# Two column blocks of the modulation matrix read in two-row pieces and multiplied on four column strips, in a one-core kernel of two transformer blocks

## What is computed

```python
# first block: a vector c modulates the block, nine vectors of 1024
mod = silu(c) @ w_ada + b_ada            # w_ada is 1024 x 9216
sh1, sc1, gt1, sh2, sc2, gt2, sh3, sc3, gt3 = split(mod, 9)
u = rmsnorm(h, g_norm_ffn1) * (1 + sc1) + sh1
h = h + 0.5 * gt1 * swiglu(u, w_ffn1_in, w_ffn1_out)
...                                       # mixing, second FFN, final norm
# second block, two layers: mixer, layer norm, routed experts, layer norm
x = layer_norm(ALPHA * x + mixer(x), ln1_g, ln1_b)
f = hier_moe(x)      # 1 of 8 groups, then 2 of its 8 experts for each token
x = layer_norm(ALPHA * x + f, ln2_g, ln2_b)
```

## Time and profile before

| | us |
|---|---|
| median of three runs | 2788.43 (2787.32 to 2788.45) |
| the profiled execution | 2787.28 |
| its span | 2785.5 |
| PE busy | 2512.2 (90%) |
| PE weight loads busy | 1814.7 (65%) |
| DVE busy | 1378.5 (49%) |
| ACT busy | 822.7 (30%) |
| POOL busy | 97.8 (4%) |

### The profile page before, as it was taken

How to read it: one execution, slowest core, us unless ns; L and a number is a source line. 1 busy time by engine, 2 the same in 40 slices (tenths; PEclk the granted TensorE clock), 3 DMA queues, 4 the chain that set the end, 5 groups by cost and what they waited for, 6 DMA issues and landing times.

```text
span 2785.5 us, 37631 instructions
## 1 busy us (share of the span) xinstructions
PE 2512.2 (90%) x14755; PEld 1814.7 (65%) x14756; DVE 1378.5 (49%) x2444; ACT 822.7 (30%) x1400; POOL 97.8 (4%) x80
## 2 busy tenths in 40 slices
PE   6999999999999999999788888888999968888886
PEld 5888888777678888787645444445765854444443
DVE  4655744634452225544664443434966475444444
ACT  3222334256232224322222112122367332121121
POOL 0100002000000000000020000003000020000000
PEclk8999999999999999999899999999999989999999
DMA  7655432401232332223389999984230449999976
GB/s 251 191 188 190 160 98 84 139 31 61 106 106 91 105 98 83 91 91 121 136 328 422 422 422 422 422 347 153 76 107 1 151 152 408 421 421 422 422 302 283
DMA packets 206763, 593.78 MB, mean 213 GB/s; under 512 B 9472, under 2 KB 133584, under 8 KB 157264
## 3 DMA queue, kind: packets, MB, share of 16 engines
q1 hardware_dynamic: 202880, 575.47, 53.9%
q0 software_dynamic: 3504, 16.63, 1.9%
q10 hardware_dynamic: 288, 0.42, 0.1%
HBM read 590.32 MB, written 7.41 MB: 215 GB/s over the span
## 4 chain that ended last, share of the span: by engine, by line
PE 65%; DMA 22%; DVE 7%; ACT 3%; issue 2%; SPq 1%; DVEq 0%; ACTq 0%
PE bank L1950 39%; DMA arena<-in_exp_w 19%; PE bank L2306 6%; PE bank L2040 4%; DMA ring<-in_exp_w 2%; PE bank L2326 1%; PE bank L2533 1%; SPq L580 1%; PE bank L2211 1%; PE bank L2430 1%; PE bank L2500 1%; DMA ring<-in_w_ada 1%; PE bank L2130 1%; DVE ring_low L1207 1%; PE bank L2275 1%
## 5 line engine op out<-in xcount | busy, mean ns | idle before, releaser
L1950 PE MATMUL bank<-parts 128*128 128x512 f32 x2624 | 816.9, 393 | 15.2 <-DVE parts L1256 9.7
L1950 PEld LDWEIGHTS bank<-parts 128*128 128x128 f32 x2624 | 492.8, 189 | 117.2 <-issue 14.8
L1950 PE MATMUL bank<-parts,ring_low 128*128 128x512 f32 x1312 | 513.4, 391 | 0.0
L1207 DVE TENSOR_TENSOR ring_low<-ring,parts 128x2048 fp32r<-128x2048 f32 x106 | 238.1, 2250 | 215.2 <-ACT parts L770 214.9
L2306 PE MATMUL bank<-ring,arena 128*32 128x256 f32 x2112 | 290.5, 433 | 57.8 <-DMA arena<-in_exp_w 57.8
L2306 PE MATMUL bank<-arena 128*32 128x256 f32 x2112 | 290.7, 433 | 30.8 <-issue 30.8
L1950 PEld LDWEIGHTS bank<-parts,ring_low 128*128 128x128 f32 x1312 | 247.7, 189 | 52.2
L770 ACT ACTIVATE parts<-ring 128x2048 fp32r<-128x2048 f32 x106 | 198.9, 1877 | 263.5 <-DMA ring<-in_w_ffn_in 108.6
L2306 PEld LDWEIGHTS bank<-ring,arena 128*32 128x32 f32 x2112 | 139.3, 120 | 122.7 <-issue 94.7
L2333 PE MATMUL bank<-parts 128*128 128x512 f32 x496 | 169.3, 447 | 43.8 <-DVE parts L1699 22.9
L1950 PE MATMUL bank<-ring_low 128*128 128x512 f32 x576 | 194.4, 396 | 1.7 <-ACT arena L1008 1.7
(11 more groups left out here) (349 smaller groups left out, 3548.4 us busy)
## 6 DMA issues: line engine op xcount, KB each, us to landing
arena<-in_exp_w SPq DMA_DIRECT2D x192, 1024.0 KB, 18.1
ring<-in_exp_w SPq DMA_DIRECT2D x192, 1024.0 KB, 18.9
ring<-in_w_ffn_in SPq DMA_DIRECT2D x44, 1024.0 KB, 6.8
ring<-in_w_ada SPq DMA_DIRECT2D x36, 1024.0 KB, 5.2
ring<-in_w_ffn_out SPq DMA_DIRECT2D x20, 1024.0 KB, 5.1
ring<-in_w_in SPq DMA_DIRECT2D x18, 1024.0 KB, 5.0
ring<-in_conv_w_in SPq DMA_DIRECT2D x12, 1024.0 KB, 5.1
ring<-in_attn_w_in SPq DMA_DIRECT2D x10, 1024.0 KB, 5.3
```

The costliest lines, as they stand in the source:

```text
L1207: TTn(ring_low[:, n, 0:nk * cols], ring[:, n, 0:nk * cols], buf.bitcast(F32), ALU.subtract)\
L1950: i = mm(o, a[:, cols[0], cols[1]], b, start=first_ and n == 0, stop=last_ and n == 2)
```

## The change

Four things are edited together.

1. *Prologue.* The eight first chunks of `w_ada` become two row tiles by 1024 columns (rows of 4 KB), four for `sc1` and then four for `sh1`. PE takes all of them: the stationary operand is a 32-column tile `CZ` whose first column is the silu vector and the rest zero, the chunk is the moving operand in halves of 512 columns, and the four products of a chunk fall on four different column strips. Of two banks, DVE copies the sums to `AROW`, and PE adds over partitions with a column of ones, eight products for a vector. PE's order becomes: chunks 0 and 1, transposes of `x`, chunks 2 and 3, the norm's spread, the sums of `sc1`, chunks 4 to 7, the sums of `sh1`. DVE writes all eight `U` tiles between the two vectors, then the low weights, then the low tiles. The stream's order of chunks stays as it was; the chunks are freed by PE's semaphore `ada_mm`.
2. *Token layout.* `XTH` and `XTL` keep the tokens' own column order, so that ACT and DVE read and write runs; the regrouping moves to `rows`, where PE's transposes read every eighth float of `XG`, and so wait for both halves of it.
3. *Layer norm.* For the last token tile DVE scales before it writes the former tile's half, and PE transposes the last tile before it takes the former tile's logits.
4. *Plan.* DVE's `rows_high` of the first turn is placed within the plan, and the last copy of the plan goes.

```diff
+        AROW = area(11264, 2, 512)
+        CZ = area(8192, KT, 32)
...
-                used = ("ada_mm", a + 1) if a < ADA_FIRST and a % 2 else ("ada_step", steps_before(a) + 8)
-                stream_a.append((tall(A["w_ada"], 256 * a, 256), KT, 256, *used))
+                if a < ADA_FIRST:
+                    stream_a.append((flat(A["w_ada"], 2 * (a % 4), 2, D * (1 - a // 4), D), 2, D, "ada_mm", a + 1))
+                else:
+                    stream_a.append((tall(A["w_ada"], 256 * a, 256), KT, 256, "ada_step", steps_before(a) + 8))
...
@@ ACT, norm @@
                     weights_high(0)
                     weights_high(1)
+                    act.wait_ge(sem("ada_mod"), ADA_FIRST)
...
             def rounded_tokens(j, t):
                 act.wait_ge(sem("xn"), 4 * j + t + 1)
-                evac(grouped(XTH, t), byrow(t), "xt")
+                evac(XTH[:, t], HT[:, t], "xt")
...
@@ DVE, layer_norm @@
+                    hurried = j in (0, 2) and t == 3
+                    if hurried:
+                        normal(j, t)
                     if t:
                         lifted(j, t - 1)
-                    normal(j, t)
+                    if not hurried:
+                        normal(j, t)
...
@@ DVE, prologue @@
-            for a in range(0, ADA_FIRST, 2):
-                ada(a, a, a // 2)
-                for done in (a - 2, a - 1) if a else ():
-                    ada_mod(done, done)
-                if a == 4:
-                    dve.wait_ge(sem("keep"), 16)
-                    roots(0)
...
+            st.did(nc.vector.memset(CZ, 0.0))
+            st.wait()
+            nc.vector.tensor_copy(CZ[:, :, 0:1], csil[:].unsqueeze(2)).then_inc(sem("ada_cz"), 1)
+
+            def vector(v):
+                dve.wait_ge(sem("ada_mm"), 4 * v + 4)
+                if v:
+                    dve.wait_ge(sem("ada_mod"), 4)
+                for h in range(2):
+                    nc.vector.tensor_copy(AROW[:, h], bank[4 + h][:]).then_inc(sem("ada_row"), 1)
+                dve.wait_ge(sem("ada_sum"), v + 1)
+                c = KT * (1 - v)
+                TTn(mod[:, c:c + KT], bank[7][:, 16 * v:16 * v + KT], par[:, PC["b_ada"] + c:PC["b_ada"] + c + KT], ALU.add)\
+                    .then_inc(sem("ada_mod"), 4)
+
+            dve.wait_ge(sem("keep"), 16)
+            roots(0)
+            vector(0)
+            dve.wait_ge(sem("ada_mod"), 4)
             modulated_gains(0)
+            dve.wait_ge(sem("rstd"), 1)
             st.wait()
+            for k in range(KT):
+                STT(out=U[:, k], in0=H[:, k], scalar=gains[:, k:k + 1], in1=bank[6][:],
+                    op0=ALU.mult, op1=ALU.mult).then_inc(sem("normed"), 1)
+            vector(1)
             weights_low(0)
             weights_low(1)
-            norm(0, lambda k: gains[:, k:k + 1], "ffn0", lambda k: mod[:, k:k + 1])
+            dve.wait_ge(sem("ada_mod"), ADA_FIRST)
+            for k in range(KT):
+                dve.wait_ge(sem("t_high"), tiles_at["ffn0"] + k + 1)
+                STT(out=UP[1][:, k], in0=U[:, k], scalar=mod[:, k:k + 1], in1=UP[0][:, k].bitcast(F32),
+                    op0=ALU.add, op1=ALU.subtract).then_inc(sem("t_low"), 1)
...
@@ DVE, plan @@
+                dve.wait_ge(sem("ln_vectors"), 32)
+                rows_high(i0)
                 st.did(TSc(LANDS[:, of_layer], at_quad, 16.0, 16.0 + 16 * QUADS * l, ALU.mult, ALU.add))
...
-                dve.wait_ge(sem("ln_vectors"), 32)
-                rows_high(i0)
                 one_turn(i0, True)
...
@@ PE, prologue @@
+            def ada_rows(a):
+
+                landed(pe, "a", ada_first[a])
+                if a == 4:
+                    pe.wait_ge(sem("ada_row"), 2)
+                w = chunk("a", ada_first[a])
+                for half in range(2):
+                    for k in range(2):
+                        at = 32 * ((2 * half + 2 * a + k) % 4)
+                        x = mm(bank[4 + half][at:at + 32, :], CZ[:, 2 * (a % 4) + k], w[:, k, 512 * half:512 * half + 512],
+                               start=(a % 4 < 2), stop=(a % 4 > 1))
                 x.then_inc(sem("ada_mm"), 1)
+            def ada_sums(v):
+
+                for half in range(2):
+                    pe.wait_ge(sem("ada_row"), 2 * v + half + 1)
+                    for q in range(4):
+                        c = 16 * v + 4 * half + q
+                        x = mm(bank[7][:, c:c + 1], AROW[:, half, P * q:P * q + P], ones[:, 0:1], start=True, stop=True)
+                x.then_inc(sem("ada_sum"), 1)
...
+            ada_rows(0)
+            ada_rows(1)
+            pe.wait_ge(sem("x_in"), 16)
...
+            ada_rows(2)
+            ada_rows(3)
+            rstd(0)
...
+            ada_sums(0)
+            for a in range(4, ADA_FIRST):
+                ada_rows(a)
+            ada_sums(1)
...
@@ PE, token_output @@
+                turn(3)
                 logits(2)
-                turn(3)
                 logits(3)
...
@@ PE, experts @@
                 def rows(i):
+                    pe.wait_ge(sem("turn_xg"), i * 2 + 2)
                     for h in range(2):
-                        pe.wait_ge(sem("turn_xg"), i * 2 + (h + 1))
                         for k in range(4):
-                            x = tp(bank[2 + h][:, P * k:P * k + P], XG[:, P * (4 * h + k):P * (4 * h + k) + P], ident)
+                            x = tp(bank[2 + h][:, P * k:P * k + P], XG[:, 4 * h + k:4 * h + k + KT * (P - 1) + 1:KT], ident)
                         x.then_inc(sem("turn_xtp"), 1)
```

More of the change, by code:

```diff
@@ L385, in build @@
         first["ada"] = 0
+        ada_first = tuple(range(ADA_FIRST))
         def ada_chunks(n):
@@ L974, in _ @@
             act.wait_ge(sem("side_tp"), 1)
-            evac(LROW[0:64], bank[7][0:64, 0:P], "side_out")
+            evac(LROW[0:64], bank[7][0:64, 64:64 + P], "side_out")
             ffn(0)
@@ L1245, in norm @@
             def norm(i, gain, parts_of=None, shift=None):
-                if i:
-                    roots(i)
+                roots(i)
                 dve.wait_ge(sem("rstd"), i + 1)
@@ L1643, in pick_weights, with rows_high @@
                     TTn(WS, EQ[:, 0], EQ[:, 1], ALU.add).then_inc(sem("turn_ws"), 1)
+                def rows_high(i):
+                    dve.wait_ge(sem("turn_xtp"), i * 2 + 2)
+                    for k in range(4, KT):
+                        x = TSc(XW[:, k], bank[3][:, P * (k - 4):P * (k - 4) + P], gpart[:, l, k:k + 1],
+                                gpart[:, 2 + l, k:k + 1], ALU.mult, ALU.add)
+                    x.then_inc(sem("turn_xwh"), 1)
                 i0 = first_turn(dve, l)
@@ L1679, in moe @@
                 seq(TSc(before_it, before_it, float(EXPERTS * LANES), None, ALU.mult))
-                seq(STT(out=BASE[:, of_layer], in0=at_quad, scalar=float(QUAD), in1=before_it, op0=ALU.mult, op1=ALU.add))
-                nc.vector.tensor_copy(PICK[:, 0:1], PICK[:, 0:1]).then_inc(sem("moe_plan"), 1)
+                STT(out=BASE[:, of_layer], in0=at_quad, scalar=float(QUAD), in1=before_it, op0=ALU.mult, op1=ALU.add)\
+                    .then_inc(sem("moe_plan"), 1)
+                dve.wait_ge(sem("moe_plan"), l + 1)
                 def next_picks(i):
@@ L1700, in rest @@
                             op0=ALU.mult, op1=ALU.subtract).then_inc(sem("turn_yl"), 1)
-                def rows_high(i):
-                    dve.wait_ge(sem("turn_xtp"), i * 2 + 2)
-                    for k in range(4, KT):
-                        x = TSc(XW[:, k], bank[3][:, P * (k - 4):P * (k - 4) + P], gpart[:, l, k:k + 1],
-                                gpart[:, 2 + l, k:k + 1], ALU.mult, ALU.add)
-                    x.then_inc(sem("turn_xwh"), 1)
                 def collect(i, start=False):
@@ L1896, in ada @@
                 x.then_inc(sem("ada_mm"), 1)
-            def ada_columns(a):
-                landed(pe, "a", a)
-                if a >= 2:
-                    pe.wait_ge(sem("ada_mod"), a - 1)
-                w = chunk("a", a)
-                for j in range(2):
-                    for k in range(KT):
-                        x = mm(bank[4 + a % 2][:, P * j:P * j + 1], w[:, k, P * j:P * j + P], csil[:, k:k + 1],
-                               start=(k == 0), stop=(k == KT - 1))
-                x.then_inc(sem("ada_mm"), 1)
+            def ada_rows(a):
[8 more added lines that the diff above has]
+                               start=(a % 4 < 2), stop=(a % 4 > 1))
+                x.then_inc(sem("ada_mm"), 1)
+            def ada_sums(v):
[5 more added lines that the diff above has]
+                x.then_inc(sem("ada_sum"), 1)
             def sums(i, k, first_, ready, n):
@@ L1929, in _ @@
             pe.wait_ge(sem("csil"), 1)
-            for a in range(0, ADA_FIRST, 2):
-                ada(a, a, half=a // 2)
-                ada_columns(a + 1)
-                if a == 2:
-                    pe.wait_ge(sem("x_in"), 16)
-                    pe.wait_ge(sem("keep"), 16)
```

(28 more changed lines are left out.)

16 lines of the change are left out of this document (5 added, 11 removed).

## The result

The changed kernel takes 2769.26 us (median of four runs, 2766.27 to 2773.85) against 2787.88 (2786.10 to 2788.45) for the kernel before on the same chip. The ratio is 0.9936, with a 95% interval of 0.9920 to 0.9951: faster by 18.6 us, where 14.9 were forecast. The profiled execution of the changed kernel took 2773.85 us (span 2772.0), which is the slowest of its four; its span is 13.5 us shorter than the one before. The four runs lie in two pairs (2766.27 and 2766.76; 2771.76 and 2773.85), and the median falls between them. In the trace the main pass of PE is now L1988 (L1950 before), a turn's transposes of gathered tokens are L2322 (L2284), its up product is L2344 (L2306), and its down product is L2364 (L2326).

What follows compares the result with a forecast made beforehand. The late modulation vector was taken to bound PE's start, then regrouping, router and expert-weight DMA the expert layers. -12 (prologue) - 2.9 (expert layers) = -14.9 from 2787.28 gave 2772.4 us, range 2765.0 to 2781.5.

Steps and rivals of the forecast that it cites:

- where 12 stood: Prologue: PE's first FFN product starts earlier, taken as a gain of 12 us between 9.0 and 13.6.
- where 2.9 stood: Expert layers together: -3.5 us in the first and +0.6 in the second, so a gain of 2.9 us.
- the bounds were 46.6 and 51.2: Prologue: PE's first FFN product starts at 46.6 us at the high clock or 51.2 at the low, against 60.23.
- The low-clock start, 51.2: Prologue: PE still at 1.2 GHz behind the transposes, a gain of 9.0 us there; 2775.4 us in all, chance 0.15.
- The first 48 products stay at 12.47 us.: First FFN: PE's first 48 products keep their duration of 12.47 us after the earlier start.
- The stall at 84.36: FFN: PE's 9.48 us wait on a `w_ada` chunk moves along with the earlier start and costs none of the gain.
- The rival that had the head start given back in the first pairs: FFN: the earlier start is lost in the first pairs, so no effect, at 2784 us; chance 0.02.
- 4.3 and 2.0 forecast: Layer norm and router: the last logits end 4.3 us earlier in the first expert layer, 2.0 in the second.
- 1.0 us a turn for the step: Expert turns: PE's eight strided loads of `XG` cost 0.12 us more each, 1.0 us a turn.
- the step is free: Expert layers: strided loads cost PE nothing, a turn costs 0.45 us, sum -8.5; 2766.8 us, chance 0.07.
- the rival of the long transposes: Expert turns: strided loads exceed the 2.5 us slack, so steady turns lengthen; 2794.6 us at 0.36 a load, chance 0.04.
- +0.6 and -0.4: First rows before turn 0 and the plan: PE's start shifts +0.6 us in the first layer, -0.4 in the second.

Runs made afterwards that it cites:

- e1: The kernel before with the prologue's edits alone, expert layers unchanged: 2778.64 us, ratio 0.9958.
- e2: The kernel before with the expert layers' edits alone (token layout, last tile's order, plan), prologue unchanged: 2782.50 us, ratio 0.9977.
- e8: e4 with DVE's low part of the first weight chunk between the second vector's copies and bias, and fifteen identity products instead of eighteen there: 2764.41 us.
- e4: The changed kernel with identity products into a spare bank in PE's two pauses, ten before and eighteen behind the second vector's sums: 2765.34 us, ratio 0.9914.
- e12: The changed kernel with all modulation pieces on one column strip instead of four: 2783.53 us, ratio 0.9981.
- e3: The changed kernel as it is, run again beside its parts on one chip: 2773.50 us, ratio 0.9938 to the kernel before.
- e6: The kernel before with the last token tile's new order alone (earlier scaling, transposes ahead of the third tile's logits): 2783.87 us, ratio 0.9985.
- e11: e10 with the added set of transposes loading its operand at a step of eight floats: 2792.73 us, ratio 1.0015.
- e10: The kernel before with a turn's eight token transposes made twice, on runs, both sets behind both gathered halves: 2794.40 us, ratio 1.0022.
- e7: The kernel before with the plan edit alone, the first turn's high tiles inside the plan: 2792.43 us, ratio 1.0013.
- e9: e8 with the first turn's high tiles put back behind the plan, as in the kernel before: 2762.06 us, ratio 0.9902.

## Why the prediction was right, and where its steps failed

The time lies in the range, and 3.1 us under the forecast. The two parts of the sum were off in opposite ways: the prologue brought 10.4 us where 12 stood, the expert layers 6.5 where 2.9 stood (e1, e2). That 10.4 is so near 12 is luck: it is the median of runs that gained some 14 and runs that gained some 6.

*PE's start.* Right in its mechanism, and earlier than both ends given: 45.73, where the bounds were 46.6 and 51.2. `x` landed at 16.2 and not at 17.3, the eight `U` tiles took 5.36 us and not 5.6, and the last tile of them ended at 36.7. Strips at 0.91 to 0.96 a chunk were the high-clock value; only the second sums (2.91) were between the two rates. A start that is bound by a landing was named as what would make the forecast wrong; it was near: in e8, where PE starts 1.9 us earlier, the landing is the bound.

*The transposes and the clock.* The low-clock start, 51.2, did not come. From 13.0 us, where the strips of chunk 1 end, to 24.54 PE ran the 32 transposes alone, and the strips right behind them were fast (0.96 us a chunk, 1.93 for chunk 1). The Trainium skill, TensorE: Matmul & The Clock Gate, Part 4: PE-mode transpose, by which they should have been slow, does not agree with this. The transposes themselves took 3.67 and 3.65 us for 16 records each in the changed kernel, 3.40 and 2.11 in e4, and 1.97 and 2.11 in e12, where 8.82 us of products end 1.5 us ahead of them. The clock column reads 1.00 through all of this, so the two rates are told by the durations alone.

*"The first 48 products stay at 12.47 us."* This step failed: 13.99, 12.84 in e3 and 13.92 in e1. Both kernels start them behind a pause of PE (7.27 us before, 5.48 after) at a clock of 0.50, and what differs is when they become fast: 2.7 us into them before, about 6 in the changed kernel. The traces don't show what sets that moment. A size that hangs on it is not a constant to be carried over; e4 shows the end that was open below, 11.16.

*The stall at 84.36 that "moves along with the start and eats nothing of the gain".* It moved along (71.10, 13.26 us earlier, 9.71 long), but in the changed kernel's trace PE's clock was 0.66 behind it and the next set took 12.49; in e1 and e3 that set took 10.91. I took a head start of PE to be worth its size at the end. In this trace it lost 1.6 us more at the end of the first FFN (a `w_ffn_out` landing 11.3 us after its issue, 9.7 before) and about 3 us in the mix stage; the faster half of e1's runs lost almost nothing. The rival that had the head start given back in the first pairs named the right kind of loss in the wrong place, and made all of it go.

*Layer norm and router.* 4.3 and 2.0 forecast, 4.6 (the lead grows from 7.0 to 11.6 us) and 2.1 (from 11.2 to 13.3) found. But the split was wrong: e6 shows the order alone gives most of it (router's end 3.9 us earlier in the first layer), and not 0.7.

*The strided loads.* The term that was mis-sized most: 1.0 us a turn for the step, measured 0.02 (e11 against e10). I had added the excess of the nearest row (309 against 188 ns, a step of four floats) to the load, and the load to the turn. The load grew by 53 ns only, and it stays under the product that runs beside it. The wait for both halves, 0.45 in the sum, came out at 0.5 (25.95 less 25.44). So "the step is free" was right about the step. Its sum was worked out wrongly: -8.5 holds neither the step nor the wait that the same sentence names. With 0.45 for each of the four turns it is -6.7, and the time 2768.6; twice the excess gives some +1, not +3; and the rival of the long transposes counts six exposed turns where the sum counts four. That -6.7 meets the 6.5 of e2 is luck again: the plan cost 3.3 us where 0.2 stood, and the layout and the order brought 9.8 where 6.9 stood without the step. The Trainium skill, SBUF — State Buffer, Door 1: The DMA port swizzle, has each access to a new line of 16 bytes pay, from which I took both steps to cost alike; the rows say 193 ns and not 309, and the measurement decides. The two rows are not of the same kind of load, though: loads on runs, too, take 140 ns at the one place and 188 at the other. DVE's regrouping pass agrees with the rule's direction: 2052 ns before, 1222 on runs, and ACT's went from 2.06 us to 1.07, as forecast.

*The plan.* "+0.6 and -0.4" for PE's start was wrong in sign for the first layer (in e7 the start comes 0.9 and 1.05 us sooner behind the router), and the price was not in that start. The text named POOL's adds behind the plan and then priced SP alone. POOL's adds lengthen DVE's next picks: e7 costs 3.3 us, and e9 gets 1.8 to 3.6 back.

The errors have one thing in common: each step was priced as if alone. The engine beside it (POOL against DVE), the work ahead of it (PE's clock) and the work that hides it (a load under a product) decided. Some 7 us of the head start are gone at the convolution in the traces of e1, e3 and the changed kernel, though not in every run. Part of that is PE's clock; why transfers take longer there stays open.

## What to carry to other kernels

When an edit lets TensorE start earlier, look for a pause just ahead of the new start: here it was paid for in the first products, and useless products in the pause that end before the real ones are a cheap way to see how much. Look at the single runs before a median is put down to a theory: it can lie where no run does. Price a longer weight load against the product that it runs under, not by itself. And when a signal is moved, list what every engine starts on it: here GpSimd's passes began 1.1 us later, the next picks some 1 us sooner, and VectorE's passes that used to lie behind them were slowed.

## What was not expected of the hardware

Useless products of PE in two pauses of 8.5 us together made this kernel 8 us faster (e4 against e3), and its runs agree within 1.3 us, where those of e3 spread by 5.4; only 2.4 of the 8 us are traced to the first products. Two-operand passes of DVE take four times as long beside POOL's passes (0.69 and 2.8 us). Eight strided weight loads of PE a turn cost no time that shows (193 ns each, under products of 276).
